# Two token tiles crossing the borders between sub-layers one behind the other

## What is computed

```python
for layer in range(2):
    h = x * (1.0 + scale) + shift          # modulation from c @ ada_w
    y = mixer_ab(h, ...) if layer == 0 else mixer_c(h, ...)   # projections, attention, @ w_out
    x = layer_norm(alpha * x + gate * y, ln_g[layer, 0], ln_b[layer, 0])
    h = x * (1.0 + scale) + shift
    y = jnp.square(jax.nn.relu(h @ mlp_w1[layer])) @ mlp_w2[layer]
    x = layer_norm(alpha * x + gate * y, ln_g[layer, 1], ln_b[layer, 1])
```

## Time and profile before

| | |
|---|---|
| median of 3 runs | 1203.57 us (1201.99 to 1203.89) |
| the profiled execution, its own time | 1208.35 us |
| its span in the trace | 1206.5 us |
| granted PE clock over the span, share of full speed | 0.912 |
| PE busy | 1028.1 us, 85% |
| DVE busy | 752.1 us, 62% |
| ACT busy | 495.0 us, 41% |
| POOL busy | 81.0 us, 7% |
| weight transfers (SP's queue) | 193.25 MB |

### The profile page before, as it was taken

The page is one execution under the profiler, slowest core; times in us unless marked ns, Lnnn a source line. Parts: engine busy times, 40 slices in busy tenths (PEclk is TensorE's granted clock), DMA queues, the critical chain, the costliest instruction groups (busy, mean ns, idle before and its releaser), DMA issues.

```text
span 1206.5 us, 14563 instructions
## 1 busy us (share of the span) xinstructions
PE 1028.1 (85%) x5726; PEld 843.1 (70%) x5726; DVE 752.1 (62%) x1105; ACT 495.0 (41%) x771; POOL 81.0 (7%) x53
## 2 busy tenths in 40 slices
PE   3696677899999688998795999969998888788886
PEld 1474455798998457776595889857887767666764
DVE  1554836777777876555766455586555476784554
ACT  1344232443442142553342344325557255436461
POOL 1000000500000040000250000010000000120000
PEclk8797788899999888999897999979999799888998
DMA  8772253668787865432686666535443155430130
GB/s 323 280 275 93 70 175 111 203 227 293 265 280 256 304 241 159 139 105 70 213 250 165 196 181 198 182 102 175 140 136 100 53 175 171 143 122 18 62 105 35
DMA packets 105303, 204.85 MB, mean 170 GB/s; under 512 B 3834, under 2 KB 38100, under 8 KB 105236
## 3 DMA queue, kind: packets, MB, share of 16 engines
q1 hardware_dynamic: 102180, 193.25, 47.6%
q0 software_dynamic: 3056, 10.67, 3.1%
HBM read 202.76 MB, written 1.15 MB: 169 GB/s over the span
## 4 chain that ended last, share of the span: by engine, by line
PE 58%; DVE 19%; DMA 8%; ACT 6%; issue 5%; POOL 2%; SPq 1%; ACTq 0%; DVEq 0%; POOLq 0%
PE bank L1348 11%; PE bank L1350 11%; PE bank L1349 11%; DVE w_lo L1467 5%; PE bank L1367 4%; DMA raw<-in_ada_w 4%; PE bank L1368 4%; PE bank L1369 4%; PE bank L1426 3%; ACT w_hi L1057 3%; PE bank L1388 2%; DVE ht_lo L1472 2%; PE bank L1252 2%; PE bank L1313 2%; ACT probs L1204 1%
## 5 line engine op out<-in xcount | busy, mean ns | idle before, releaser
L1467 DVE TENSOR_TENSOR w_lo<-raw,w_hi 128x2048 fp32r<-128x2048 f32 (+2 forms) x138 | 319.2, 2326 | 200.6 <-ACT w_hi L1057 199.9
L1057 ACT ACTIVATE w_hi<-raw 128x2048 fp32r<-128x2048 f32 (+2 forms) x138 | 255.3, 1859 | 210.4 <-PE bank L1350 90.7
L1348 PE MATMUL bank<-w_lo,ht_hi 128*128 128x512 f32 (+1 forms) x544 | 226.8, 417 | 50.3 <-DVE ht_lo L1472 25.0
L1350 PE MATMUL bank<-w_hi,ht_lo 128*128 128x512 f32 (+1 forms) x544 | 219.9, 404 | 0.0
L1349 PE MATMUL bank<-w_hi,ht_hi 128*128 128x512 f32 (+1 forms) x544 | 219.9, 404 | 0.0
L1367 PE MATMUL bank<-ht_hi,w_lo 128*128 128x256 f32 x512 | 148.4, 290 | 18.7 <-DVE w_lo L1467 14.4
L1348 PEld LDWEIGHTS bank<-w_lo,ht_hi 128*128 128x128 f32 x544 | 108.8, 200 | 77.7 <-issue 43.5
L1368 PE MATMUL bank<-ht_lo,w_hi 128*128 128x256 f32 x512 | 147.3, 288 | 0.0
L1369 PE MATMUL bank<-ht_hi,w_hi 128*128 128x256 f32 x512 | 147.2, 287 | 0.0
L1350 PEld LDWEIGHTS bank<-w_hi,ht_lo 128*128 128x128 f32 x544 | 108.3, 199 | 24.0
L1349 PEld LDWEIGHTS bank<-w_hi,ht_hi 128*128 128x128 f32 x544 | 109.2, 201 | 21.9 <-issue 0.2
(11 more groups left out here) (185 smaller groups left out, 1210.1 us busy)
## 6 DMA issues: line engine op xcount, KB each, us to landing
raw<-in_mlp_w SPq DMA_DIRECT2D x64, 1024.0 KB, 5.8
raw<-in_ada_w SPq DMA_DIRECT2D x48, 1024.0 KB, 5.5
raw<-in_a_w_in SPq DMA_DIRECT2D x16, 1024.0 KB, 5.3
raw<-in_c_w_in SPq DMA_DIRECT2D x12, 1024.0 KB, 5.4
raw<-in_b_w_in SPq DMA_DIRECT2D x10, 1024.0 KB, 5.1
raw<-in_ple_w_gate SPq DMA_DIRECT2D x8, 1024.0 KB, 4.9
raw<-in_ab_w_in SPq DMA_DIRECT2D x4, 1024.0 KB, 13.8
raw<-in_ab_w_out SPq DMA_DIRECT2D x4, 1024.0 KB, 5.6
```

The costliest lines, as they stand in the source:

```text
L1057: nc.scalar.activation(split_parts(n)[0], raw_tile(t), ACT.Copy).then_inc(high_done, 1)
L1348: nc.tensor.matmul(dst, a_hi[:, c, rows], lo[:, k, :], start=it["first"] and k == 0, stop=False)
L1350: mm = nc.tensor.matmul(dst, a_lo[:, c, rows], hi[:, k, :], start=False, stop=it["last"] and k == it["kc"] - 1)
L1467: nc.vector.tensor_tensor(lo, raw_tile(split[n]), hi.bitcast(F32), ALU.subtract).then_inc(low_done, 1)
```

## The change

Every border is crossed by token tile 0 first and tile 1 behind it.

- `norm_ln` and the "ln" item work on one token tile; the small operations of `rsqrt_one` are done once for each tile (11 in place of 12 for both).
- `across` (items "turn_rows") turns one token tile: 2 items of 4 transposes, into one bank each. For t = 0 ACT does both affines (4 operations of 128x128 and one rounding copy of 128x512 each), for t = 1 ACT does one and DVE the other. DVE writes `ht_lo`.
- `last_tiles`, `halves`, `entered`, and the end of `down`: the last one or two weight tiles of a sub-layer, and the first two of the next, are each passed over twice, once per token tile (items "tokens" with `ts`, and "up_tokens"). For this a fourth rounded slot, `w_spare`, lies over `probs`; `junk` moves onto `biased`.
- The first up tiles of an MLP are computed with token rows on the partitions ("up_tokens"), copied by ACT to `biased`, and turned by 8 more transposes ("turn_hidden").
- Of the four ada_product tiles of a border, two stand ahead of the first pass and two between or after (`extra`, `ada_tiles`). In the MLP of layer 0, the 4 ada_sum tiles of the last down projection move to the up projections.
- POOL waits at every border, border 3 too, for the last cut of token tile 1. At border 3 "resid" and "rms" stand ahead of the last item of q[0], where "resid" stood ahead and "rms" behind.

```diff
--- before.py
+++ after.py
+        def entered(s):
+
+            bk = banks((0, 1))
+            two = [tile(w1[:, :, h * 256:(h + 1) * 256], KD, 256, "split", h == 1) for h in range(2)]
+
+            def part(t):
+                for h in range(2):
+                    if t:
+                        again(two[h])
+                    it = add("up_tokens", tile=two[h], h=h, t=t, banks=bk, cut=cuts["ht", t], ahead_by=1 if h == t else 0 if t == 0 else 1)
+                    if t == 0:
+                        it["half"] = tick("half")
+                it["end"] = "biased"
+
+            across(s, 0, (4, 5), ("act", "act"))
+            norm_ln(s - 1, 1)
+            if layer < 2:
+                ada_tiles(1, 7)
+            part(0)
+            across(s, 1, (4, 5), ("act", "dve"))
+            if layer < 2:
+                ada_tiles(1, 7)
+            part(1)
+            pair[0] = 1
+            return [(b, used + 1) for b, used in bk]
...
+                    if copied and h == 0:
+                        over = add("turn_hidden", after=copied, banks=banks((0, 1)), buf=0, c0=0, job=tick("job"))
+                        ended(over, over["banks"])
...
+            if g < 3:
+                return
+            for t in range(T):
+                for h in range(2):
+                    if t:
+                        again(parted[h][0])
+                    it = add("tokens", tile=parted[h][0], kc=4, width=512, lhs=("hid", 1), off=h * 4, banks=yb[1], ts=(t,),
+                             first=False, last=h == 1, cut=hid_cut[3], enter=False, ahead_by=3 if (t, h) == (0, 0) else 2 if h == 0 else 1)
+                    if t == 0:
+                        it["half"] = tick("half")
+                it["end"], it["ends"] = ("y_ln", 1, 2 * layer + 1), (t,)
+                if t == 0:
+                    norm_ln(2 * layer + 1, 0)
...
-            up(1), down(0, each), up(2), down(1, each), up(3)
+            up(1, (3,)), down(0, each), up(2, (3,)), down(1, each), up(3, (1, 3))
             columns(2, 0)
             columns(2, 1)
-            down(2, each), down(3, each)
-            ada_tiles(4, 3)
+            down(2, each), down(3)
...
+    def norm_ln(s, t):
+
+        rows_of[s, t] = add("ln", s=s, t=t, rows=rows())
+
+    def across(s, t, places, engines):
+
+        for half in range(2):
+            it = add("turn_rows", s=s, t=t, a=4 * half, banks=banks((places[half],)), job=tick("job"), wait=rows_of[s - 1, t]["rows"],
+                     engine=engines[half])
+            place = places[half] % 4
+            it["emptied"] = cut_of.get(place, 0)
+            if it["engine"] == "act":
+                it["high"] = tick("high")
+            cut_of[place] = tick("cut")
+        cuts["ht", t] = (count["cut"] - 1, count["cut"])
+        cuts["ht"] = cuts["ht", t]
+        if t == 1:
+            for i in range(T):
+                rows_of[s - 1, i]["cut"] = count["cut"]
+
+    def last_tiles(s):
+
+        y[0](1, 3, look=3)
+        y[1](1, 2, ts=(0,))
+        norm_ln(s, 0)
+        y[1](1, 2, ts=(1,))
+        ada_tiles(2, 7)
+
+    def halves(first, s, extra, ends=True):
+
+        across(s, 0, (0, 1), ("act", "act"))
+        if extra:
+            ada_tiles(2, 3)
+        norm_ln(s - 1, 1)
+        first(0, 1, ts=(0,), cut=cuts["ht", 0][0])
+        early = first(1, 0, ts=(0,), cut=cuts["ht", 0][1], spare=True, ends=ends)
+        across(s, 1, (4, 5), ("act", "dve"))
+        if extra:
+            ada_tiles(2, 3)
+        first(0, 1, ts=(1,))
+        late = first(1, 1, ts=(1,), ends=(1,) if ends else (0, 1))
+        late["half"] = early["half"]
+        return late
...
-    split_rows("xhat", KD, "ht", last_rows, ("affine", 4))
...
-    q[0](0)
-    stream_rows()
-    q0 = q[0](1)
-    norm_rms(0)
+    q0 = halves(q[0], 4, False, ends=False)
+    plan.insert(len(plan) - 1, {"kind": "resid", "s": 3})
+    tick("ssq", 4)
+    plan.insert(len(plan) - 1, {"kind": "rms", "ssq": count["ssq"], "i": 0})
...
+        until = min(max(given[1], t["n"] + t["look"] + 1), len(split))
+        given[0].extend(split[given[1]:until])
+        given[1] = until
...
+        w_spare = over(probs, 0, "w_spare", [P, TILE], F32R)
...
-                    pool.wait_ge(rows_ready, norms[s]["rows"] - T + t + 1)
-                    if "cut" in norms[s]:
-                        pool.wait_ge(split_done, norms[s]["cut"])
+                    pool.wait_ge(rows_ready, norms[s, t]["rows"])
+                    pool.wait_ge(split_done, norms[s, t]["cut"])
...
+                elif kind == "turn_hidden":
+                    enter(it["after"])
+                    enter(it["banks"])
+                    for c in range(4):
+                        b, _ = it["banks"][c // 2]
+                        for t in range(T):
+                            o = (c % 2) * S + t * P
+                            mm = nc.tensor.transpose(bank[b][:, o:o + P], biased[:, t, c // 2, (c % 2) * P:(c % 2 + 1) * P], ident)
+                    mm.then_inc(job_done, 1)
...
-                    for t in range(T):
-                        link(nc.vector.bn_aggr(meanvar[:, t, :], stats[:, t, :, :]))
-                    link(nc.vector.tensor_scalar(small[:, 0, 0:T], meanvar[:, :, 1], LN_EPS, None, ALU.add))
-                    rsqrt(small[:, 0, 0:T], T)
-                    for t in range(T):
-                        nc.vector.tensor_scalar(u[:, t, :], u[:, t, :], meanvar[:, t, 0:1], rstd[:, t:t + 1],
-                                                ALU.subtract, ALU.mult).then_inc(rows_ready, 1)
-                        dve.wait_ge(rows_ready, it["rows"] - T + t + 1)
+                    t = it["t"]
+                    link(nc.vector.bn_aggr(meanvar[:, t, :], stats[:, t, :, :]))
+                    link(nc.vector.tensor_scalar(small[:, 0, 0:1], meanvar[:, t, 1:2], LN_EPS, None, ALU.add))
+                    rsqrt_one(rstd[:, 0:1], small[:, 0, 0:1])
+                    nc.vector.tensor_scalar(u[:, t, :], u[:, t, :], meanvar[:, t, 0:1], rstd[:, 0:1], ALU.subtract, ALU.mult).then_inc(rows_ready, 1)
...```

Two places show what moves. First DVE at border 3, from the last split of the activations to the RMS factors. Before:

```order
L1472 TENSOR_TENSOR ht_lo<-full,ht_hi 128x512 x2
L1467 TENSOR_TENSOR w_lo<-raw,w_hi 128x2048 x2
L1717 TENSOR_TENSOR x<-u,g_row 128x1024
L1718 TENSOR_TENSOR x<-x,b_row 128x1024
L1467 TENSOR_TENSOR w_lo<-raw,w_hi 128x2048
L1724 TENSOR_TENSOR small<-ssq 128x2
L1725 TENSOR_SCALAR small<-small 128x2
```

More of the change, by code:

```diff
@@ L149, in banks, with tile, again @@
         return got
-    def tile(view, kc, cols, kind):
-        tiles.append({"view": view, "kc": kc, "cols": cols, "kind": kind, "n": tick(kind) - 1})
+    def tile(view, kc, cols, kind, spare=False, look=2):
+        tiles.append({"view": view, "kc": kc, "cols": cols, "kind": kind, "n": tick(kind) - 1, "spare": spare, "look": look,
+                      "turned": 2 * sum(i["kind"] == "probs" for i in plan)})
         return tiles[-1]["n"]
+    def again(n):
+        t = next(t for t in tiles if t["kind"] == "split" and t["n"] == n)
+        tiles.remove(t)
+        tiles.append(t)
     def job(kind, pairs=None, **k):
@@ L319, in mlp, with ended, up @@
         w2 = R["mlp_w2"][layer].rearrange("(k p) n -> p k n", p=P)
-        yb = {n: banks((4 + 2 * n, 5 + 2 * n)) for n in range(2)}
+        yb = {}
         hid_cut = {}
-        enter = {0: True, 1: True}
-        need = cuts["ht"]
-        def up(g, ada=()):
+        parted = {}
+        def ended(it, bk):
+            it["end"] = "hidden"
+            it["high"] = tick("high")
+            it["emptied"] = max(cut_of.get(b, 0) for b, _ in bk)
+            tick("cut", 2)
+            for b, _ in bk:
+                cut_of[b] = count["cut"]
+        def entered(s):
[20 more added lines that the diff above has]
+            return [(b, used + 1) for b, used in bk]
+        def up(g, ada=(), copied=None):
             for j in range(2):
+                if copied and j == 0:
+                    continue
                 bk = banks()
@@ L1147, in _ @@
                             act.wait_ge(rms_ready, scale[0] + 1)
[L1148 removed]
+                        for t in it["ends"]:
+                            b, used = it["banks"][t]
                             came(act, it, t)
```

209 lines of the change are left out of this document (139 added, 70 removed).

## The result

The change takes 1211.76 us (median of 5 runs, 1210.45 to 1214.99) against 1203.89 in the same session (5 runs), a ratio of 1.0068 with a 95% interval of 1.0045 to 1.0090. On another chip it was 1.0045 (1.0026 to 1.0063). So it is slower, by 0.26% at the least over both intervals. The forecast was 1207.5, slower with 0.50.

The account below looks back on a forecast made before the run. PE was taken to bound the kernel, and DVE wherever PE stands still. Border terms -1 - 7 + 2.3 + 9.5 = +3.8 us on the profiled 1208.35 gave 1212.2, as a median 1207.4, rounded to 1207.5; range 1197.5 to 1214.

Parts of the forecast that it names:

- four signs for "right": k[0] waits 8 us or more behind rms; near_bias E+62 to E+67; v[0] 5 to 10 us nearer; border 0 within 4.
- signs for "wrong": k[0] by E+28; POOL's x at border 2 ahead of E+18; passes' clock near 1.00 or 0.5; DVE wait in up projections.
- rival C: Up projections of layer 0: moved ada tiles starve one w_lo, up to 2.6 us; 1210 in all; chance 0.09.
- The common piece: Every border: next sub-layer's first two weight tiles done E+20.5 to E+25, middle E+23; E ends a sub-layer's last product.
- Border 0: First border: two tiles done at 26 to 28.5 against 28.9, bank reuse costing up to 4; taken as -1 (-4 to +4).
- The moved sums: Up projections of layer 0: the moved ada_sum tiles cost nothing, as DVE has 38% free over the span.
- Border 1: Second border: q[0] done 13.5 us earlier, partly lost to a w_lo behind the rope; -7 (-10 to -4).
- Border 2: Third border: POOL starts later, its chain to near_bias is not shortened, PE waits there; +2.3 (+0.7 to +5.5).
- Border 3: Fourth border: k[0]'s w_lo behind resid and rms, +6.5, and a slow PE restart, 3; +9.5 (+5 to +12).
- Rival A: Border passes keep full clock, two tiles done at E+20.5; -5.4 us, 1198, faster; chance 0.29.
- Rival B: Four short waits of each border bring half clock in every pass; +13, 1216.5; chance 0.12.

Follow-up runs that it names:

- the first experiment: The change, with ACT and DVE preparing both weight tiles of k[0] ahead of resid, squares and rms at border 3: 1209.31 us, 1.0022 of before.

## Why the prediction was right, and where its terms were off

The forecast was slower, 1207.5 in 1197.5 to 1214; 1211.76 is 4 us above it and inside. Its mechanism, gains at the first borders paid back at the fourth by an order of DVE, is what the runs show. That its sum fits as well as it does is luck: the five stretches in which it had terms give -2.8 + 3.3 - 4.4 - 0.5 + 8.1 = +3.7 us, against +3.8, while the single terms are off by 1.4 to 3.3 us, up and down. Of the four signs for "right" two came (the wait of 8.80 us behind rms, border 0 within 4) and two were missed by a little (near_bias at E+61.0 and not E+62 to E+67, v[0] 4.4 us nearer to E and not 5 to 10); of the signs for "wrong" the one of rival C came. By its terms, in traces:

- **The common piece** gave q[0] at E+23 in E+20.5 to E+25; measured 24.2 to 25.1, at the late end, and not for one reason. At border 3 it was the clock, as said: t = 0's rows were ready at E+2.0 and its products started at E+5.9, but the two passes took 7.8 and 7.3 us and not 5.4. At border 1 the clock was 1.00 in the passes; there a second w_lo, that of the spare slot, stood ahead of t = 0's statistics (404.20 and 406.41), where the text had one, and with it and the ada_product work the products started at E+10.2.
- **Border 0**, -1: measured -2.8.
- **The moved sums**, costed at nothing under a DVE with room: measured +3.3, of which 2.6 us are waits of PE for w_lo (1.10, 1.19, 0.30). This step failed: the mean of 38% free over the span did not cover this stretch. Rival C had priced this, one wait of up to 2.6, at a chance of 0.09; it came together with the forecast.
- **Border 1**, -7 (-10 to -4): measured -4.4. The wait for w_lo behind the rope was as said (6 to 9 us: 8.63; w_lo at E+39.2 where E+35 to 38 was said). The slow start behind the wait came too: ten products 0.43 us apart and not 0.23, some 2 us. What the text did not see is that the whole gain is the sums': they give -10.8 alone, and the crossing +6.4. Nor did it see that the sums' gain at border 1 and their cost in the up projections belong together: from the gate products to v[0] this trace wins 1.1 us only (217.8 against 218.9).
- **Border 2**, +2.3: measured -0.5. POOL's start was right (E+19.9 in 18.7 to 21.8). The step that failed is that nothing behind it is shortened: POOL's operations met fewer of DVE's (13.8 us in place of 16.2), and the transfer behind them was quicker by 2.6 us; near_rev, slower by 2.5, took back a part. The text had named the first of these ("a part may come back") and given it little.
- **Border 3**, +9.5 (+5 to +12): measured +8.1, with k[0] at E+33.5 (said: 31.3 to 34.3) and 8.80 us of wait (8 to 10). POOL's two operations and resid took 6.8 us together (806.57 to 813.33), where 7.2 was said. The size was right, the cause named too narrowly. Taking w_lo out from behind rms (the first experiment) moved the wait to v[0]; what sets it is the chain to rms. POOL's new wait is 3 us of it; how the rest of the 9 us is shared between resid's place and the weights' was not run apart.
- **Rival A** needed short waits and a full clock. The clock did hold in the passes of border 1, and the waits for u were 5.17 and 2.17 us; even so border 1 gave -4.4 and not its -9.6, and its border 3 (+7) stands beside a measured +8.1. The order behind the passes decided, not the clock in them.
- **Rival B**, the clock low in every pass, is out: 0.94 to 1.00 at borders 0 to 2 (the first pass and the second together). By the Trainium skill ("TensorE: Matmul & The Clock Gate", section "HAM oscillation — how this bites in real kernels") bursts with waits between fall back each time. Of the passes the trace agrees at border 3, where 7.8 us of products behind 5.9 us with 1.07 busy ran at 0.70, and for the first 8 to 10 products at borders 0 and 2 (0.21 us apart, then 0.12), but not at border 1. It agrees behind the long waits, too, where after 8.63 and 8.80 us of idle the first ten or so products came 0.43 us apart and the later ones 0.23.
- The rule of "SBUF — State Buffer", section "SBUF: two separate sides", of the Trainium skill (a VectorE operation with two SBUF inputs and a GpSimd operation exclude each other) holds in the trace: the rope's tmp_b takes 2.6 us beside POOL and 0.4 alone and its last sum 2.72 and 0.69, and POOL's x takes 3.21 beside resid and 2.40 alone.

The median came 4.3 above the sum's 1207.4, the traces only 2.0 apart where 3.8 was forecast. The runs of one kernel spread by 5 to 9 us, so one profiled execution for each is not exact to that; where the rest of the 8 us between the medians lies stays open.
